# One exponential over a head's whole row, and its place in the step order, in attention B of blocks 2 and 3

## What is computed

```
score  = where(admissible, sum_h w[t,h] * relu(q_idx[t,h] . k_idx[s]), NEG)
keep   = top-256 keys of each query
logits = q . k * 64^-0.5 + t5_bias          # 8 heads, one shared k and v of width 64
p      = softmax(where(kept and admissible, logits, NEG))
o_b    = p @ v
```

## Time and profile before

| | us |
|---|---|
| median of 3 runs | 3290.53 (3290.22 to 3292.28) |
| the profiled execution | 3296.36 |
| its span | 3294.5 |
| PE busy | 3218.5 |
| DVE, POOL, ACT busy | 1930.1, 1819.1, 1443.8 |
| mean granted TensorE clock, share of full | 0.997 |

### The profile page before, as it was taken

How to read it: one execution, slowest core, us unless ns; L and a number is a source line. 1 busy time by engine, 2 the same in 40 slices (tenths; PEclk the granted TensorE clock), 3 DMA queues, 4 the chain that set the end, 5 groups by cost and what they waited for, 6 DMA issues and landing times.

```text
span 3294.5 us, 43302 instructions
## 1 busy us (share of the span) xinstructions
PE 3218.5 (98%) x15976; PEld 2696.8 (82%) x15976; DVE 1930.1 (59%) x3494; ACT 1443.8 (44%) x2610; POOL 1819.1 (55%) x1261
## 2 busy tenths in 40 slices
PE   8999999999999999999999999999999999999998
PEld 6888878878788888888888888888888789888887
DVE  3236747648565656567666766767868778621112
ACT  3324435435454534345454534736655367420001
POOL 4555554454456666655666664166666721566665
PEclk9999999999999999999999999999999999999999
DMA  5745454355524333323433332063333400333332
GB/s 159 209 138 172 115 165 138 104 153 155 190 67 155 112 106 104 116 93 112 167 106 108 96 119 93 1 233 100 96 103 115 160 15 1 137 118 98 96 103 96
DMA packets 446561, 388.98 MB, mean 118 GB/s; under 512 B 20976, under 2 KB 376560, under 8 KB 445712
## 3 DMA queue, kind: packets, MB, share of 16 engines
q1 hardware_dynamic: 424912, 341.99, 34.0%
q10 hardware_dynamic: 21440, 44.22, 3.6%
HBM read 323.37 MB, written 62.78 MB: 117 GB/s over the span
## 4 chain that ended last, share of the span: by engine, by line
PE 85%; DVE 6%; ACT 4%; issue 2%; POOL 1%; DMA 1%; ACTq 0%; SPq 0%; DVEq 0%; POOLq 0%
PE BANK L913 19%; PE BANK L914 19%; PE BANK L915 19%; PE LP L913 3%; PE LP L915 3%; PE LP L914 3%; PE BANK L1138 3%; PE LP L1122 2%; PE BANK L1153 2%; PE LP L1123 2%; PE LP L1023 2%; PE LP L1022 2%; PE BANK L1155 2%; PE BANK L1164 1%; ACT PThi L1445 1%
## 5 line engine op out<-in xcount | busy, mean ns | idle before, releaser
L863 POOL TENSOR_TENSOR WLO<-WRAW,WHI 128x1024 fp32r<-128x1024 f32 x456 | 1114.5, 2444 | 38.1
L861 POOL TENSOR_SCALAR WHI<-WRAW 128x1024 fp32r<-128x1024 f32 x456 | 508.1, 1114 | 1026.0 <-PE BANK L915 845.8
L913 PE MATMUL BANK<-H2hi,WHI 128*128 128x512 f32 x1376 | 542.0, 394 | 4.7 <-POOL WLO L863 4.7
L914 PE MATMUL BANK<-H2lo,WHI 128*128 128x512 f32 x1376 | 537.1, 390 | 0.0
L915 PE MATMUL BANK<-H2hi,WLO 128*128 128x512 f32 x1376 | 536.6, 390 | 0.0
L913 PE MATMUL BANK<-HThi,WHI 128*128 128x512 f32 (+1 forms) x1024 | 404.1, 395 | 2.0 <-DVE QS L1782 2.0
L914 PE MATMUL BANK<-HTlo,WHI 128*128 128x512 f32 (+1 forms) x1024 | 400.0, 391 | 0.0
L915 PE MATMUL BANK<-HThi,WLO 128*128 128x512 f32 (+1 forms) x1024 | 399.8, 390 | 0.0
L1515 ACT ACTIVATE MASK<-SCD,THR 128x896 bf16<-128x896 f32 (+5 forms) x186 | 282.0, 1517 | 243.7 <-DVE THR L1842 215.5
L913 PEld LDWEIGHTS BANK<-H2hi,WHI 128*128 128x128 f32 x1376 | 259.0, 188 | 57.2 <-issue 6.7
L915 PEld LDWEIGHTS BANK<-H2hi,WLO 128*128 128x128 f32 x1376 | 258.8, 188 | 55.2
(11 more groups left out here) (294 smaller groups left out, 6666.2 us busy)
## 6 DMA issues: line engine op xcount, KB each, us to landing
WRAW<-in_w_in SPq DMA_DIRECT2D x124, 512.0 KB, 4.4
WRAW<-in_w_ffn_gate SPq DMA_DIRECT2D x88, 512.0 KB, 3.8
WRAW<-in_w_ffn_up SPq DMA_DIRECT2D x88, 512.0 KB, 3.8
WRAW<-in_w_ffn_down SPq DMA_DIRECT2D x88, 512.0 KB, 3.4
qsp<-QS SPq DMA_DIRECT2D x32, 512.0 KB, 5.7
gates<-GS ACTq DMA_DIRECT2D x64, 256.0 KB, 2.2
WRAW<-in_w_out SPq DMA_DIRECT2D x32, 512.0 KB, 4.3
GL<-gates ACTq DMA_DIRECT2D x48, 256.0 KB, 5.0
```

The lines of the kernel that those rows point to most:

```text
L861: nc.gpsimd.tensor_scalar(hi, raw, 1.0, 1.0, ALU.mult, ALU.mult).then_inc(w_hi, 1)
L863: nc.gpsimd.tensor_tensor(lo, raw, hi.bitcast(f32), ALU.subtract).then_inc(w_split, 1)
L913: nc.tensor.matmul(dst, whi, mhi, start=first, stop=False)
L914: nc.tensor.matmul(dst, whi, mlo, start=False, stop=False)
```

## The change

In `exps` the loop over chunks is gone: a head's exponentials are one instruction over its whole row, in place, with one sum, which goes to `RS`. `exp_times` places the two instructions of a pair at i-5 and i-3 where the row has over 1024 columns (blocks 2 and 3); where it has not (blocks 0 and 1) the times are those of before. `whole_sums` is left for mixer A alone, so POOL's addition of the second sum and DVE's wait for it are gone in attention B. The transposes of every group wait for the whole rows of both heads.

```diff
--- before.py
+++ after.py
@@ -415,9 +415,8 @@
             times = [first_at(b, "a", p) - 4 for p in range(PAIRS)] if b == 0 else []
             for p in range(PAIRS):
                 i, count = first_at(b, "b", p), len(groups(b, "b", p))
-                times += [i - (4 if count > 3 else 3), i - 2]
-                if len(chunks_of(pair_heads(b, "b", p)[0][1])) > 1:
-                    times += [i, i + (2 if count > 6 else 1)]
+                wide = key_tiles(b, "b", p // 4)[0] * P > LGW
+                times += [i - 5, i - 3] if wide else [i - (4 if count > 3 else 3), i - 2]
             return rising(times)
 
         def due(times, i):
@@ -763,14 +762,11 @@
                     nc.gpsimd.tensor_tensor(SN[:, i % 4, :], SINK[:, h0:h0 + 4], MX[:, i % 4, :], ALU.subtract
                                             ).then_inc(sink_ready, made(sink_ready, u))
 
-                def whole_sums(kind, q):
+                def whole_sums(q):
                     j, hs = q // 2, slice(4 * (q % 2), 4 * (q % 2) + 4)
-                    if kind == "b" and len(chunks_of(units(b, "b")[4 * q])) == 1:
-                        return
-                    last = (b, "a", 2 * q + 1) if kind == "a" else (units(b, "b")[4 * q + 3], 1)
-                    pool.wait_ge(probs, n(probs, last))
+                    pool.wait_ge(probs, n(probs, (b, "a", 2 * q + 1)))
                     nc.gpsimd.tensor_tensor(RS[:, j, hs], RS[:, j, hs], ES[:, j, hs], ALU.add
-                                            ).then_inc(sums_whole, made(sums_whole, (b, kind, q)))
+                                            ).then_inc(sums_whole, made(sums_whole, (b, q)))
 
                 def combine(i):
 
@@ -831,8 +827,8 @@
                     nc.gpsimd.tensor_tensor(FOLD[:, :], IDENT[:, 0:HD], IDENT[:, HD:P], ALU.add).then_inc(fold_set, 1)
                 for i in range(FIRST, len(all_groups(b)) + AFTER):
                     for kind, q in quads(b):
-                        if i == quad_end(b, kind, q):
-                            whole_sums(kind, q)
+                        if kind == "a" and i == quad_end(b, kind, q):
+                            whole_sums(q)
                     for u in range(PAIRS // 2):
                         if b == 0 and i == first_at(b, "a", 2 * u + 1) - 6:
                             add_sink(u)
@@ -1132,7 +1128,7 @@
                         pe.wait_ge(probs, n(probs, (b, "a", p)))
                     else:
                         for _, u, _ in pair_heads(b, kind, p):
-                            pe.wait_ge(probs, n(probs, (u, grp[0] * P // LGW)))
+                            pe.wait_ge(probs, n(probs, u))
                     for e, t in enumerate(grp):
                         for h in range(2):
                             last = nc.tensor.transpose(dst[:, 2 * e + h, :], probabilities(b, kind, p, h, t), IDENT[:, :])
@@ -1407,15 +1403,14 @@
                             act.wait_ge(o_ready, n(o_ready, (b, "a", p // 2 + 1)))
                         if b and p == 0:
                             act.wait_ge(near_kept, n(near_kept, (b, PAIRS // 2 - 1)))
-                        for s in range(len(chunks_of(heads[0][1]))):
-                            for i, u, _ in heads:
-                                _, _, j, h0 = u
-                                c, cw = chunks_of(u)[s]
-                                act.wait_ge(negmax, n(negmax, u))
-                                lg, slot = LGB[b][i % LGRING[b]][:, c:c + cw], i % LGRING[b]
-                                nc.scalar.activation(lg, lg, ACT.Exp, bias=NMB[:, slot, 0:1],
-                                                     accum_out=(ES if s else RS)[:, j, h0:h0 + 1]).then_inc(probs, made(probs, (u, s)))
-                                yield
+                        for i, u, _ in heads:
+                            _, _, j, h0 = u
+                            act.wait_ge(negmax, n(negmax, u))
+                            slot = i % LGRING[b]
+                            lg = LGB[b][slot][:, 0:key_tiles(b, "b", j)[0] * P]
+                            nc.scalar.activation(lg, lg, ACT.Exp, bias=NMB[:, slot, 0:1],
+                                                 accum_out=RS[:, j, h0:h0 + 1]).then_inc(probs, made(probs, u))
+                            yield
 
                 def x_copy(kind, q):
                     act.wait_ge(values_done, n(values_done, last_group(b, kind, 2 * q + 1)))
@@ -1945,8 +1940,8 @@
 
                 def invert(kind, q):
                     j, hs = q // 2, slice(4 * (q % 2), 4 * (q % 2) + 4)
-                    if kind == "a" or len(chunks_of(units(b, "b")[4 * q])) > 1:
-                        dve.wait_ge(sums_whole, n(sums_whole, (b, kind, q)))
+                    if kind == "a":
+                        dve.wait_ge(sums_whole, n(sums_whole, (b, q)))
                     nc.vector.reciprocal(RS[:, j, hs], RS[:, j, hs]).then_inc(inverted, made(inverted, (b, kind, q)))
 
                 def split_low(e):
```

## The result

The changed kernel takes 3344.23 us (median of 4 runs, 3342.3 to 3346.4), the kernel before beside it 3290.38: 1.0157 of its time (95% interval 1.0144 to 1.0169), 54 us slower. The profiled execution took 3343.3 us, its span is 3341.5, 47.0 more than the span before.

A forecast was written before the change was run, and what follows sets the result against it. PE was taken as the bound, with score matmuls waiting for DVE's masks. Losses of 22.4 + 12.7 + 0.8 + 0.4 + 7.7 + 5.6, less about 1, gave 48.6 us on 3290.53: 3339 us, range 3306 to 3358 (own range 3325 to 3352).

The forecast's parts named there:

- The chain of a pair of 8 groups: Block 3, pairs 8 to 14: late exponentials delay masks that PE's score matmuls need, 7 x 3.2 = 22.4 us lost.
- Pairs of 7 groups: Block 3, pairs 1 to 7: `PThi` late ahead of a mask, 2.1 or 1.6 us a pair, 12.7 us lost.
- Ends of block 3: First and last pairs of block 3's attention B: 0.4 us lost at the start, 0.8 at the end.
- Block 2: Attention B of block 2: 7.7 us lost in pairs of 6 groups, 5.6 in pairs of 5, nothing at its end.
- the 0.4 us a pair: Block 2, pairs of 6 groups: 0.4 us back because short second exponentials no longer stand ahead of a `PThi`.
- The sums: POOL's additions of `ES` to `RS` and DVE's wait go: no cost or gain, at most 0.2 us at each block's end.
- Rival 1: Blocks 2 and 3: head 0's longer exponential is absorbed, so delays don't stack; 31 us lost, 3321 us; chance 0.17.
- Rival 2: Stages of blocks 2 and 3: stalls bring on half-clock stretches of PE, 24 us more, 3363 us; chance 0.09.
- signs of being wrong: Stages keep their length, new PE waits name another releaser, block 2 loses more than block 3, or granted clock falls inside the stages.
- Rival 3: Faster: head 1's `NMB` comes 0.75 us earlier, PE loses nothing and gains 4.6 + 1.2 and some 3 us: 3282; chance 0.09.
- The signs: ACT waits for `NMB`, PE for `MXB`, about once a pair; block 3's stage some 35 us longer, block 2's some 13.

The follow-up runs named there:

- sums_kept: The changed kernel with one POOL addition per quad in blocks 2 and 3 put back, and DVE's wait for it ahead of the reciprocal: 3345.49 us against 3292.73.
- head0_sooner: The changed kernel with head 0's exponential at i-6 instead of i-5 in block 3's pairs of 8 groups alone: 3335.26 us against 3293.58 for the kernel before.
- halves_placed: The changed kernel's places (i-5, i-3) with the instructions of before: two chunks a head, second sum and POOL's addition: 3372.8 us against 3293.58 for the kernel before.
- chunks_early: The kernel before with only the first chunk's exponentials one step earlier, at i-5 and i-3, in blocks 2 and 3: 3326.83 us against its 3293.58.
- whole_late: The changed kernel with its whole-row exponentials at i-4 and i-2 instead of i-5 and i-3, blocks 2 and 3: 3296.03 us against 3293.58 for the kernel before.

## Why the prediction was right

3339 us was forecast and 3344.2 measured; the forecast's own range was 3325 to 3352. The mechanism is shown; that the number came so near is in part luck. With the falls of the clock taken out, the terms of the sum, as measured below, come to some 44 us (21.0 + 12.6 - 1.9 + 11.0 + 2.4 - 0.9) and not 48.6, most of all because the ends of the stages gained. Four more falls, which the sum did not have, brought the growth of the stages to 50, and the median of before lies 6 us below the execution with which they are compared.

- *The chain of a pair of 8 groups* held to within 0.05 us at each link (the table above). Forecast 22.4 us for seven pairs; the seven measured distances from pair 8's first transposes to pair 15's grew by 24.2, two falls of the clock (3 us) among them: 21 without.
- *Pairs of 7 groups:* forecast 12.7 us, measured 15.8 (pairs 1 to 7), two falls of 1.6 among them: 12.6 without.
- *Ends of block 3:* I forecast a loss of 1.2 us. Both ends gained: the first pair's stretch is 1.88 us shorter and the last's 0.55. But these are mixed with the clock: before had its fall in the first pair and the changed kernel has one in the last. sums_kept, which issues the same but for POOL's additions, has it the other way round: with a fall the first pair is 0.30 shorter than before, and without one the last is 1.60 shorter. So the gain is 0.3 at the start and 1.6 at the end. That it comes from the second chunks' exponentials, which no longer stand among the last steps, is not shown by itself.
- *Block 2* was forecast at +13 and came out at +12.6, but by errors that cancel. Pairs 8 to 14 lost 12.6 and not 7.7: one fall of the clock lies there (sums_kept has none in them and lost 11.0), and the 0.4 us a pair that I had given back never came. Pairs 1 to 7 lost 2.4 and not 5.6. Perhaps the delay hides where PE had been waiting for head 1's exponential; no run shows it. Its two ends gained 2.4, where I had put nothing; some 1.5 of it is before's fall of the clock in the first pair, which the changed kernel has not.
- *The sums* at nothing: shown by sums_kept.
- *Rival 1* (the delays don't stack, 3321) is out by head0_sooner and by the table: the `NMB` comes 1.10 us later than before (4.92 against 3.82), so head 0's 1.12 reach it in full.
- *Rival 2* (the clock) was a part of the truth beside the forecast, not instead of it: four more falls in the two stages, some 6 us, against the 24 that I had given it. The forecast's sum had none of them, and one of its own signs of being wrong, a granted clock that falls inside the stages, did show (0.96 in block 3). The row that I had set against this rival is weak: its window in block 0 ends at 957 us, and from 957 to 962 the granted clock of the kernel before is 0.66. The Trainium skill (TensorE: Matmul & The Clock Gate, "A second HAM failure mode: psum-queue depth-cycling") describes a kernel in which frequent short idle times of PE between groups of matmuls made the clock swing. The traces agree by and large, with 6 falls in the two stages where PE stalls by 1 to 3 us a pair against 2 in the kernel before, and 15 in halves_placed; but chunks_early, whose waits for a mask last up to 1.5 us, has 2 as well. That the stalls bring on the falls is not shown further than that.
- *Rival 3* (faster) needed the `NMB` 0.75 us earlier. It came later by all that head 0 added, and ACT waited up to 2.0 us for it. What this rival promised, fewer waits for exponentials, came in block 2 (4.6 to 0.8 us) and not in block 3, where they grew from 1.2 to 3.5 over the whole stage.
- *The signs:* ACT's wait for `NMB` (8 times in seven pairs, 14.9 us), block 3's stage some 35 us longer (37.5) and block 2's some 13 (12.6), and 1.9 us for 1920 columns came as said. PE was to wait for `MXB` once a pair, by 2 to 3 us; it waits twice (0.98 and 1.85 us in pair 10), since the mask of step i-4 is late as well.
- *Slips in the working:* PE's own waits in the middle of block 3 were not all for `MXB`, as two more of 0.4 us together were for ACT's copy of an output; and the chances of the outcomes outside 3306 to 3358 add up to 0.23 and not to 0.2 or less. Neither moves the sum.

What stays open: what head 1's wait for `NMB` costs by itself, since no run takes away that wait alone. For the lengths there is a check: chunks_early, with exponentials 0.75 us shorter for each head, loses 1.4 us a pair of 8 groups and the changed kernel without its falls 3.0, which fits two lengths that count in full. Open are also the 6 us by which the profiled execution of before stood above its median, and why the 0.4 us of the pairs of 6 groups did not come back.

## What to carry to other kernels

When engines step through a pipeline in program order, an instruction's cost can be set by what is queued behind it on its own engine and who waits for that. Here the same two exponentials a pair, with 17.5 us less of ACT's busy time in the two stages, cost 54 us in steps that come before a mask, and 2.5 or nothing when they or the masks stand one step away. Before moving work earlier, mark the steps in which a following engine owes something that the bound engine waits for; put long instructions into those steps, behind the copy that feeds the debt, not into the step ahead of them; and keep two steps between an instruction and a result that passes through two other engines.

## What the runs showed of the hardware

The length of an exponential on 128 rows of float32 stayed on one line up to 2048 columns: 2008 ns at 2048 and 1902 at 1920, where the line through 406 at 128 and 1152 at 1024 gives 2005 and 1898. The kernels with the longest stalls of PE had the most falls of TensorE's clock: 15 in the two stages of halves_placed and 6 in those of the changed kernel, against 2 before, 2 in chunks_early and none in whole_late, whose windows have 1.00. Each costs 1.3 to 1.6 us, close to the 1.7 by which 3.41 us at half clock delay an engine that is busy throughout.
